# A two-block fp32 transformer kernel: sums with a 0/1 matrix as split fp32r products, both heads of a pair side by side

## The chip, the core and the metric

One Trainium2 chip, one of its cores. The metric is the device time of one execution of the whole program, in microseconds (us); the kernel before took 2313.67 us, the median of three runs (2313.24 to 2315.27).

## The reference, cut to what matters

Two layers of a first block (feed-forward, mixer, feed-forward), then two layers of a second block that the change doesn't touch. The sequence is 256 tokens, the width 1024, with 8 heads of 128. The mixer has two branches. The delta branch runs a gated delta rule and norms its output per head:

```python
o_a = gated_delta_rule_chunked(q, k, v, g, beta).transpose(0, 2, 1, 3)
o_a = rmsnorm(o_a, dn_out_norm) * jax.nn.silu(dn_z...)
```

The stick branch is an attention whose weights need, for each query, a sum over the keys behind each key:

```python
log_1mb = jnp.where(causal, -jax.nn.softplus(z), 0.0)
survive = lax.cumsum(log_1mb, axis=3, reverse=True) - log_1mb
weights = jnp.where(causal, jnp.exp(jax.nn.log_sigmoid(z) + survive), 0.0)
```

All arithmetic has the accuracy of fp32. Weights of products are cut in two fp32r parts (high and low, `hi` and `lo`), and a product is three matmuls of parts.

## The kernel before, in words

**Queues.** SyncE loads weight units of 1 MB into a ring of three buffers `raw`. ScalarE copies each into `hi` in fp32r (L1313), GpSimd subtracts and writes `lo`, four instructions of 128x512 a unit (L539), and TensorE multiplies. Each engine has one order of work, written out by hand, and waits on semaphores.

**Mixer.** The dependent steps of the delta rule and of the stick branch are short, so TensorE fills the time between them with parts of weight units: a unit is 48 matmuls of 256 columns and is cut in four parts of 12. `DELTA_PLAN` and `SB_PLAN` say how many parts stand behind which step; they are computed from the weights `DELTA_WEIGHT` and `SB_WEIGHT`. In the stick branch the steps of one pair of heads are `z` (scores), `tri` (sums) and `pv` (output). Pair 0 has 12 parts behind `z` and 8 behind `tri`; pairs 1, 2 and 3 have 3 behind each `z`, and 2, 3 and 2 behind `tri`; none stands behind `pv`.

**Stick, one pair.** TensorE writes the scores of head i to bank 4 + i (L938, L939). ScalarE takes the absolute value, Exp and Ln (L1520 to L1522). VectorE forms max(z, 0) + soft (L2152) and multiplies with a mask of 0 and -1 (`sbneg`, L2153), 768 columns each, and signals `nsp`. TensorE does the square sums of the next pair (`pre`, L794), waits for `nsp`, and adds the sums: per head three fp32 matmuls of 256, 128 and 128 columns with the 0/1 matrices `tri` and `ones` stationary (L948 to L950). VectorE then forms the exponent (L2157), ScalarE does Exp (L1535), TensorE the output (L958, L959).

**Delta, output norm, one pair.** There are four pairs a layer. ScalarE squares the output into `sq` (L1500), VectorE adds a term (L2133) and signals `osq`. TensorE sums over partitions with `ones` in fp32, two matmuls of 256 columns (L839), the first thing of the next pair's work on TensorE. ScalarE takes the root (L1460). On VectorE `started` stands behind L2133 (L2061, L2064), then the steps of the next pair.

An fp32 matmul is two records in the trace, each with a weight load. The helper `halve` cuts a tile in two fp32r parts: a copy (L1916), a wait for it, a subtraction (L1917).

```python
def halve(h, l_, src):
    own.link(V.tensor_copy(h, src))
    return tt(l_, src, h.bitcast(F32), ALU.subtract)
```

Of the kernel before, what the change touches and what calls it, by code (L numbers as in the profile page):

```python
# [25 lines left out]
P = 128  # L26
D = 1024
S = 256
# [37 lines left out]
          "sbneg", "sbadd", "cosa", "sina", "cosb", "sinb", "scan"]  # L66
CONST_W = {**{f"inv{n}": 64 for n in range(6)}, "half": 64, "sbneg": 384, "sbadd": 384, "cosa": 256, "sina": 256, "cosb": 256, "sinb": 256, "scan": 256}
# [194 lines left out]
def build_program(nc, a, const, out):  # L262
    ctx = ExitStack()
    with ctx:
# [36 lines left out]
        beta_r, g_r, eg_r = (sb(n, [HEADS, S]) for n in ("beta_r", "g_r", "eg_r"))  # L301
# [244 lines left out]
        def _(pe):  # L546
# [424 lines left out]
            def mixer1(l, b, q):  # L971
# [24 lines left out]
                for n, row in enumerate((beta_r[:, :], g_r[:, :], sq[0:HEADS, 0, 0:S], sq[0:HEADS, 1, S:2 * S])):  # L996
# [307 lines left out]
        def _(act):  # L1304
# [203 lines left out]
            def stick(l, c):  # L1508
# [11 lines left out]
                own.link(fn(soft.rearrange("p (i n) -> p i n", i=2), ps[:, 4:6, 0:384], ACT.Abs))  # L1520
# [366 lines left out]
        def _(dve):  # L1887
# [134 lines left out]
            def delta(l):  # L2022
# [60 lines left out]
                for c in range(NPAIR):  # L2083
# [49 lines left out]
                    tt(o2, o2, ps[:, 6:8, S:2 * S], ALU.add).then_inc(dl_dve, 1)  # L2133
# [44 lines left out]
            def mixer1(l, b):  # L2178
                h8 = slice(0, HEADS)
                y, e = sq[h8, 0, 0:S], sq[h8, 0, S:2 * S]  # L2180
                gates = ps[h8, A_AT % 2, S:2 * S]
# [378 lines left out]
```

## Time and profile before

| | |
|---|---|
| median of three runs | 2313.67 us |
| the profiled execution, from its first to its last instruction | 2311.9 us |
| TensorE matmul busy | 2261.3 us, 98% |
| TensorE weight load busy | 2061.2 us, 89% |
| VectorE busy | 1068.2 us, 46% |
| ScalarE busy | 1090.0 us, 47% |
| GpSimd busy | 1698.7 us, 73% |
| granted TensorE clock, mean | 0.999 of full speed |

The span stands 1.8 us below the median: what lies around the instructions isn't in the profile. PE is a matmul, PEld a weight load, DVE is VectorE, ACT ScalarE, POOL GpSimd. In brackets behind a row stands the idle time of its engine just before it, and whose work ended it. Matmuls are pipelined: the spacing of their starts tells what one costs, not its duration.

### The profile page before, as it was taken

What the parts mean: (1) busy time and instruction counts of PE and PEld (TensorE: products, weight loads), DVE (VectorE), ACT (ScalarE), POOL (GpSimd) and SP (SyncE); (2) the same over time, 40 slices, a digit from 0 to 9 for tenths busy, and PEclk for the clock granted to TensorE, in tenths of its full rate; (3) what the DMA queues carried; (4) which work ended last, traced back from release to release, by engine and by line L of the source; (5) the groups of instructions that cost most, each with busy time, mean ns of one, the idle gap of its engine ahead of it and who ended that gap; (6) DMA issues with size and microseconds to landing.
All of it is one profiled execution on the core that took longest, in us unless ns stands there. A gap on an engine that the chain in (4) does not pass through costs nothing.

```text
span 2311.9 us, 41644 instructions
## 1 busy us (share of the span) xinstructions
PE 2261.3 (98%) x16621; PEld 2061.2 (89%) x16621; DVE 1068.2 (46%) x1873; ACT 1090.0 (47%) x1319; POOL 1698.7 (73%) x1340
## 2 busy tenths in 40 slices
PE   8999999999999999999999999999999999999998
PEld 7888999999988888898999998889898888898887
DVE  3334656323333333365553233333635765534766
ACT  4335444465433533454444734345654335565333
POOL 6998655556799899874554678996567997555996
PEclk9999999999999999999999999999999999999999
DMA  7554533334565555543333445664334555333553
GB/s 239 192 197 148 165 110 111 119 101 146 166 200 186 178 193 188 190 156 108 108 118 108 142 158 176 193 208 137 110 121 143 191 187 180 117 104 119 198 197 119
DMA packets 312365, 359.91 MB, mean 156 GB/s; under 512 B 18660, under 2 KB 291104, under 8 KB 312096
## 3 DMA queue, kind: packets, MB, share of 16 engines
q1 hardware_dynamic: 311866, 357.59, 47.6%
q8 instruction: 102, 1.67, 0.3%
q10 hardware_dynamic: 358, 0.33, 0.0%
q14 instruction: 39, 0.32, 0.0%
HBM read 356.84 MB, written 1.05 MB: 155 GB/s over the span
## 4 chain that ended last, share of the span: by engine, by line
PE 89%; DVE 6%; ACT 3%; POOL 1%; issue 1%; DMA 0%; SPq 0%; ACTq 0%; DVEq 0%
PE ps L755 23%; PE ps L566 21%; PE ps L598 17%; PE ps L603 9%; PE ps L632 4%; PE ps L885 1%; PE ps L867 1%; PE ps L1154 1%; PE ps L648 1%; POOL sb_lo L539 1%; PE ps L888 1%; PE ps L619 1%; PE ps L1206 1%; PE ps L794 1%; PE ps L989 1%
## 5 line engine op out<-in xcount | busy, mean ns | idle before, releaser
L539 POOL TENSOR_TENSOR sb_lo<-sb_raw,sb_hi 128x512 fp32r<-128x512 f32 (+1 forms) x1336 | 1698.5, 1306 | 594.9 <-ACT sb_hi L1313 593.5
L1313 ACT ACTIVATE sb_hi<-sb_raw 128x2048 fp32r<-128x2048 f32 (+3 forms) x341 | 639.4, 1877 | 740.2 <-PE ps L603 358.4
L598 PE MATMUL ps<-sb_hT,sb_hi 128*128 128x512 f32 x1792 | 426.0, 390 | 0.0
L598 PEld LDWEIGHTS ps<-sb_hT,sb_hi 128*128 128x128 f32 x1792 | 332.7, 188 | 66.7
L755 PE MATMUL ps<-sb_hT,sb_hi 128*128 128x256 f32 x2304 | 309.0, 287 | 4.5 <-DVE sb_hT L2162 2.8
L755 PEld LDWEIGHTS ps<-sb_hT,sb_hi 128*128 128x128 f32 x2304 | 284.9, 191 | 10.6 <-DVE sb_hT L2162 3.2
L603 PEld LDWEIGHTS ps<-sb_hT,sb_lo 128*128 128x128 f32 x1792 | 229.8, 191 | 8.7
L1910 DVE TENSOR_TENSOR sb_yinv<-ps,sb_row 128x512 f32<-128x512 f32 x112 | 77.5, 692 | 337.2 <-PE ps L603 336.4
L603 PE MATMUL ps<-sb_hT,sb_lo 128*128 128x256 f32 x1792 | 232.4, 283 | 0.0
L566 PE MATMUL ps<-sb_hi,sb_o_h 128*128 128x512 f32 x560 | 219.8, 392 | 0.4 <-DVE sb_o_l L1917 0.4
L566 PE MATMUL ps<-sb_hi,sb_o_l 128*128 128x512 f32 x560 | 218.7, 390 | 0.0
L566 PE MATMUL ps<-sb_lo,sb_o_h 128*128 128x512 f32 x560 | 218.0, 389 | 0.0
L755 PE MATMUL ps<-sb_hT,sb_lo 128*128 128x256 f32 x1152 | 158.2, 285 | 0.0
L755 PEld LDWEIGHTS ps<-sb_hT,sb_lo 128*128 128x128 f32 x1152 | 145.5, 191 | 1.3
L566 PEld LDWEIGHTS ps<-sb_lo,sb_o_h 128*128 128x128 f32 x560 | 105.1, 188 | 22.4
L566 PEld LDWEIGHTS ps<-sb_hi,sb_o_h 128*128 128x128 f32 x560 | 105.4, 188 | 21.0 <-DVE sb_o_l L1917 0.8
L566 PEld LDWEIGHTS ps<-sb_hi,sb_o_l 128*128 128x128 f32 x560 | 105.4, 188 | 19.2
L1904 DVE TENSOR_TENSOR ps<-ps,sb_row 128x512 f32<-128x512 f32 x134 | 92.7, 692 | 52.6 <-PE ps L566 19.0
L1916 DVE CAST sb_o_h<-ps 128x512 fp32r<-128x512 f32 x82 | 56.7, 691 | 107.8 <-PE ps L566 105.1
L566 PE MATMUL ps<-sb_hT,sb_hi 128*128 128x256 f32 (+1 forms) x520 | 96.3, 284 | 3.2 <-issue 2.0
L632 PE MATMUL ps<-sb_hT,sb_hi 128*128 128x256 f32 x448 | 90.3, 294 | 7.9 <-DVE sb_hT L1898 7.7
L566 PEld LDWEIGHTS ps<-sb_hT,sb_hi 128*128 128x128 f32 (+1 forms) x520 | 80.6, 187 | 4.6 <-issue 4.5
(402 smaller groups left out, 3355.5 us busy)
## 6 DMA issues: line engine op xcount, KB each, us to landing
sb_raw<-in_ffn_w_in SPq DMA_DIRECT2D x88, 1024.0 KB, 5.1
sb_raw<-in_w_in SPq DMA_DIRECT2D x78, 1024.0 KB, 5.2
sb_raw<-in_ffn_w_out SPq DMA_DIRECT2D x44, 1024.0 KB, 4.9
sb_raw<-in_ffn_w_up SPq DMA_DIRECT2D x44, 1024.0 KB, 5.1
sb_raw<-in_ffn_w_down SPq DMA_DIRECT2D x22, 1024.0 KB, 4.9
sb_raw<-in_w_out SPq DMA_DIRECT2D x16, 1024.0 KB, 5.2
sb_raw<-in_w_branch_a SPq DMA_DIRECT2D x8, 1024.0 KB, 5.1
sb_raw<-in_w_branch_b SPq DMA_DIRECT2D x8, 1024.0 KB, 5.2
```

Of the source, the lines that this page charges most:

```text
L539: ins = nc.gpsimd.tensor_tensor(lo[:, slot, c], raw[:, slot, c], hi[:, slot, c].bitcast(F32), ALU.subtract)
L566: ins = mm(dst, s, m, start=first and n == 0, stop=last and n == 3 * len(pairs) - 1)
L598: mm(ps[:, bank + i, :].rearrange("p (h n) -> p h n", h=2), wh[:, c, i * P:(i + 1) * P], hT_both[:, :, c, :], start=c == 0, stop=False, sk ...
L603: ins = mm(ps[:, bank + i, 0:S], wl[:, c, i * P:(i + 1) * P], hT_h[:, c, :], start=False, stop=c == KB - 1, skip_group_check=True)
L619: ins = nc.tensor.transpose(ps[:, bank, i * S + t * P:i * S + (t + 1) * P], x[:, t, k * P:(k + 1) * P], ident)
L632: ins = mm(ps[:, bank, i * S:(i + 1) * S], wt[:, c, i * P:(i + 1) * P], h[:, c, :], start=(i, c, n) == (0, 0, 0), stop=(c, n) == (KB - 1, ...
L648: ins = mm(ps[:, bank, t * S:(t + 1) * S], o[:, (c + UNSCALED_AT) % KB, tt_], wt[:, c, :], start=(t, c, n) == (0, 0, 0), stop=(c, n) == (K ...
L755: ins = mm(dst, left, right, start=at == 0, stop=of_low and k == KB - 1, skip_group_check=True)
L1313: fn(hi[:, slot, 0:width], raw[:, slot, 0:width], ACT.Copy).then_inc(hi_ready, 1)
L1904: return tt(v, v, over(row[:], 2), ALU.mult)
L1910: tt(t, low, over(row[:], 2), ALU.mult)
L1916: own.link(V.tensor_copy(h, src))
```

## The change

The stationary matrices become `-tri` and `-ones` in fp32r (`signs`, made once from the constants). The moving operand is cut by `halve` into two fp32r parts of 768 columns (`parts`), both heads of a pair side by side, so that one matmul serves both heads: for a pair two of 512 columns and four of 256 take the place of the six fp32 ones. The sign sits in the stationary matrix, so the mask is 0/1 (`before`), and VectorE multiplies only the two diagonal blocks of each head, 256 columns an instruction. The scores of a pair are laid out flat over banks 4 and 5; the number of their matmuls stays. L2157 becomes two instructions, of 512 and of 256 columns. The output sums of the delta branch are cut in the same way: `halve` over 512 columns, then four fp32r matmuls of 256 columns for two fp32 ones. To make room, `beta_r`, `g_r`, `eg_r` and the scan mask move into `quad`; the scan mask is made by three memsets a layer, and 640 columns of constants are no longer loaded.

```diff
@@ output sums, TensorE
                     for i in range(2):
-                        ins = mm(ps[:, 6 + i, S:2 * S], cc("ones"), sq[:, 0, i * S:(i + 1) * S], start=True, stop=True)
+                        for j in range(2):
+                            ins = mm(ps[:, 6 + i, S:2 * S], minus_ones, parts[:, j, i * S:(i + 1) * S], start=j == 0, stop=j == 1)
@@ stick, TensorE
                 wv("nsp")
-                for i in range(2):
-                    n0 = rsf[:, 384 * i:384 * i + S]
-                    n1 = rsf[:, 384 * i + S:384 * (i + 1)]
-                    mm(ps[:, 4 + i, 0:S], cc("tri"), n0, start=False, stop=False, skip_group_check=True)
-                    mm(ps[:, 4 + i, P:S], cc("ones"), n1, start=False, stop=False, skip_group_check=True)
-                    ins = mm(ps[:, 4 + i, S:S + P], cc("tri"), n1, start=False, stop=True, skip_group_check=True)
+                early, late = parts[:, :, 0:512], parts[:, :, 512:768]
+                behind = ps[:, 4, :].rearrange("p (i n) -> p i n", i=2)[:, :, P:S]
+                for j in range(2):
+                    mm(ps[:, 4, :], minus_tri, early[:, j, :], start=False, stop=False, skip_group_check=True)
+                for j in range(2):
+                    mm(behind, minus_ones, late[:, j, :].rearrange("p (i n) -> p i n", i=2), start=False, stop=j == 1, skip_group_check=True)
+                for j in range(2):
+                    ins = mm(ps[:, 5, 0:S], minus_tri, late[:, j, :], start=False, stop=j == 1, skip_group_check=True)
@@ output sums, VectorE
-                    tt(o2, o2, ps[:, 6:8, S:2 * S], ALU.add).then_inc(dl_dve, 1)
+                    own.link(tt(o2, o2, ps[:, 6:8, S:2 * S], ALU.add))
+                    halve(parts[:, 0, 0:512], parts[:, 1, 0:512], sq[:, 0, :]).then_inc(dl_dve, 1)
@@ stick, VectorE
-                own.link(stt(out=pair(neg), in0=ps[:, 4:6, 0:384], scalar=0.0, in1=pair(soft), op0=ALU.max, op1=ALU.add))
-                tt(pair(neg), pair(neg), over(cc("sbneg"), 2), ALU.mult).then_inc(sb_dve, 1)
+                own.link(stt(out=rate, in0=ps[:, 4:6, :].rearrange("p b n -> p (b n)")[:, 0:768], scalar=0.0, in1=soft, op0=ALU.max, op1=ALU.add))
+                for square in (pair(rate[:, 0:512])[:, :, 0:P], pair(rate[:, 512:768])):
+                    ins = tt(square, square, over(cc("before"), 2), ALU.mult)
+                own.link(ins)
+                halve(parts[:, 0, :], parts[:, 1, :], rate).then_inc(sb_dve, 1)
@@ mixer1, VectorE
+                own.link(V.memset(scan, 1.0))
+                for c in range(S // CHUNK):
+                    ins = V.memset(scan[:, c * CHUNK:c * CHUNK + 1], 0.0)
+                own.link(ins)
...
+                if l == 0:
+                    for i, name in enumerate(("tri", "ones")):
+                        ts(signs[:, i, :], cc(name), -1.0, None, ALU.mult)
```

## Rows read from the trace of the kernel before

**Rows 1.** The page, busy time of each engine over the span.

```profile
PE 2261.3 (98%) x16621; PEld 2061.2 (89%) x16621; DVE 1068.2 (46%) x1873; ACT 1090.0 (47%) x1319; POOL 1698.7 (73%) x1340
```

**Rows 2.** The chain that ended last: start us, us, what, and how many instructions.

```profile
51.57 3.65 PE ps L598 x16
...
582.22 5.76 PE ps L781 x48
```

**Rows 3.** Timeline of TensorE, stick stage, first layer: start us, us, engine, line, operation.

```profile
524.46 0.59 PE L948 MATMUL ps<-sb_rs,sb_const 128*128 128x256 f32 x2
...
526.13 1.68 PE L755 MATMUL ps<-sb_o_h,sb_lo 128*128 128x256 f32 x12
...
537.74 0.59 PE L948 MATMUL ps<-sb_rs,sb_const 128*128 128x256 f32 x2
...
551.30 0.70 PE L948 MATMUL ps<-sb_rs,sb_const 128*128 128x256 f32 x2 [0.40 <-DVE sb_rs L2153]
```

**Rows 4.** Timeline of VectorE, the same stage.

```profile
522.29 1.23 DVE L2153 TENSOR_TENSOR sb_rs<-sb_rs,sb_const 128x768 f32<-128x768 f32 x1
...
535.57 0.96 DVE L2153 TENSOR_TENSOR sb_rs<-sb_rs,sb_const 128x768 f32<-128x768 f32 x1
...
550.29 0.96 DVE L2153 TENSOR_TENSOR sb_rs<-sb_rs,sb_const 128x768 f32<-128x768 f32 x1
```

**Rows 5.** Timeline of GpSimd, the same stage.

```profile
518.90 10.73 POOL L539 TENSOR_TENSOR sb_lo<-sb_raw,sb_hi 128x512 fp32r<-128x512 f32 x8
...
530.13 5.03 POOL L539 TENSOR_TENSOR sb_lo<-sb_raw,sb_hi 128x512 fp32r<-128x512 f32 x4 [0.51 <-ACT sb_hi L1313]
...
551.14 5.00 POOL L539 TENSOR_TENSOR sb_lo<-sb_raw,sb_hi 128x512 fp32r<-128x512 f32 x4 [2.73 <-ACT sb_hi L1313]
```

**Rows 6.** One line's instructions: times, ns min/median/max, first and last start.

```profile
L2055 DVE TENSOR_TENSOR sb_levels<-sb_levels,sb_const x16: 418/1341/1550, 265.2 to 1206.5; 64x256 f32<-64x256 f32 x16
```

**Rows 7.** Groups of VectorE's instructions by shape, 1600 to 1660 us.

```profile
L1917 DVE TENSOR_TENSOR sb_hT<-sb_zT,sb_hT 128x768 fp32r<-128x768 f32 x1 | 1.0, 959 | 0.0
...
L1916 DVE CAST sb_hT<-sb_zT 128x768 fp32r<-128x768 f32 x1 | 0.6, 559 | 0.0
```

**Rows 8.** Timeline of TensorE at the output sums of pairs 0 to 3.

```profile
316.55 1.13 PE L839 MATMUL ps<-sb_sq,sb_const 128*128 128x256 f32 x4 [0.47 <-DVE sb_sq L2133]
...
372.00 1.06 PE L839 MATMUL ps<-sb_sq,sb_const 128*128 128x256 f32 x4
...
433.06 1.03 PE L839 MATMUL ps<-sb_sq,sb_const 128*128 128x256 f32 x4
...
484.26 1.03 PE L839 MATMUL ps<-sb_sq,sb_const 128*128 128x256 f32 x4
```

**Rows 9.** Timeline of VectorE at the same four places.

```profile
315.81 0.69 DVE L2133 TENSOR_TENSOR sb_sq<-sb_sq,ps 128x512 f32<-128x512 f32 x1
...
371.19 0.69 DVE L2133 TENSOR_TENSOR sb_sq<-sb_sq,ps 128x512 f32<-128x512 f32 x1
...
430.75 0.69 DVE L2133 TENSOR_TENSOR sb_sq<-sb_sq,ps 128x512 f32<-128x512 f32 x1
...
480.49 0.69 DVE L2133 TENSOR_TENSOR sb_sq<-sb_sq,ps 128x512 f32<-128x512 f32 x1 [2.98 <-ACT sb_sq L1500]
```

**Rows 10.** Timeline of GpSimd at three of them.

```profile
311.52 5.40 POOL L539 TENSOR_TENSOR sb_lo<-sb_raw,sb_hi 128x512 fp32r<-128x512 f32 x4 [6.97 <-ACT sb_hi L1313]
...
369.53 5.46 POOL L539 TENSOR_TENSOR sb_lo<-sb_raw,sb_hi 128x512 fp32r<-128x512 f32 x4 [0.49 <-ACT sb_hi L1313]
...
484.75 1.29 POOL L539 TENSOR_TENSOR sb_lo<-sb_raw,sb_hi 128x512 fp32r<-128x512 f32 x1 [3.21 <-ACT sb_hi L1313]
```

**Rows 11.** Timeline of VectorE, start of the mixer, first layer.

```profile
210.96 1.66 DVE L2187 SCALAR_TENSOR_TENSOR sb_qT<-ps,sb_vec,sb_row 128x256 f32<-128x256 f32 x4 [2.36 <-ACT sb_row L1355]
...
222.81 0.88 DVE L1988 TENSOR_SCALAR sb_qT<-ps,sb_vec 128x256 f32<-128x256 f32 x2 [3.94 <-PE ps L989]
```

**Rows 12.** Sums of a stretch: us, busy of each engine, granted clock, DMA share, GB/s.

```profile
1640.00:1650.00 10.00, 8.61 (x54) 7.74 (x53) 8.53 (x17) 5.38 (x19) 7.52 (x5) 0.83 0.43 135
```

More of the change, by code:

```diff
@@ L65 @@
 CONSTS = ["ident", "ones", "halves", "tri", "rot", "chunk", "half", "inv0", "inv1", "inv2", "inv3", "inv4", "inv5",
-          "sbneg", "sbadd", "cosa", "sina", "cosb", "sinb", "scan"]
-CONST_W = {**{f"inv{n}": 64 for n in range(6)}, "half": 64, "sbneg": 384, "sbadd": 384, "cosa": 256, "sina": 256, "cosb": 256, "sinb": 256, "scan": 256}
+          "before", "sbadd", "cosa", "sina", "cosb", "sinb"]
+CONST_W = {**{f"inv{n}": 64 for n in range(6)}, "half": 64, "sbadd": 256, "cosa": 256, "sina": 256, "cosb": 256, "sinb": 256}
 CONST_AT, _w = {}, 0
@@ L98, in constants @@
     before = (j < i).astype(np.float32)
-    full = np.concatenate([before, np.ones((P, P), np.float32), before], axis=1)
-    put("sbneg", -full)
-    put("sbadd", np.where(full > 0, 0.0, -1e30).astype(np.float32))
+    put("before", before)
+    put("sbadd", np.concatenate([np.where(before > 0, 0.0, -1e30), np.zeros((P, P))], axis=1).astype(np.float32))
     def table(d_rot):
@@ L300, in build_program @@
         vec2 = sb("vec2", [P, 3 * P])
-        beta_r, g_r, eg_r = (sb(n, [HEADS, S]) for n in ("beta_r", "g_r", "eg_r"))
+        beta_r, g_r, eg_r, scan = (quad[0:HEADS, i, 0:S] for i in range(4))
+        signs = sb("signs", [P, 2, P], F32R)
+        minus_tri, minus_ones = (signs[:, i, :] for i in range(2))
+        parts = sb("parts", [P, 2, 768], F32R)
         select = sb("select", [P, HEADS], F32R)
@@ L954, in stick @@
                 for i, h in enumerate(heads):
-                    w0 = sqf[:, 384 * i:384 * i + S]
-                    w1 = sqf[:, 384 * i + S:384 * (i + 1)]
+                    w0 = sqf[:, i * S:(i + 1) * S]
+                    w1 = sqf[:, 512 + i * P:512 + (i + 1) * P]
                     hh = slice(h * P, (h + 1) * P)
@@ L995, in mixer1 @@
                 pe.wait_ge(rows_dve, ROWS_DVE.at(l, "beg"))
-                for n, row in enumerate((beta_r[:, :], g_r[:, :], sq[0:HEADS, 0, 0:S], sq[0:HEADS, 1, S:2 * S])):
+                for n, row in enumerate((beta_r, g_r, sq[0:HEADS, 0, 0:S], sq[0:HEADS, 1, S:2 * S])):
                     for t in range(ST):
@@ L1459, in output_roots @@
                     act.wait_ge(dl_pe, DELTA_PE.at(NPAIR * l + c, "osum"))
-                    own.link(fn(two(rs[:, 0, :]), ps[:, 6:8, S:2 * S], ACT.Ln, bias=eps_t[:, 1:2], scale=1.0 / P))
+                    own.link(fn(two(rs[:, 0, :]), ps[:, 6:8, S:2 * S], ACT.Ln, bias=eps_t[:, 1:2], scale=-1.0 / P))
                     fn(rs[:, 0, :], rs[:, 0, :], ACT.Exp, scale=-0.5).then_inc(dl_act, 1)
@@ L1518, in stick @@
                 wp("z")
-                own.link(fn(soft.rearrange("p (i n) -> p i n", i=2), ps[:, 4:6, 0:384], ACT.Abs))
+                own.link(fn(soft, ps[:, 4:6, :].rearrange("p b n -> p (b n)")[:, 0:768], ACT.Abs))
                 own.link(fn(soft, soft, ACT.Exp, scale=-1.0))
@@ L2203, in mixer1 @@
                 freed(l, B_AT)
-                own.link(tt(beta_r[:, :], beta_r[:, :], cc("ones")[h8, 0:1].to_broadcast([HEADS, S]), ALU.add))
-                own.link(V.reciprocal(beta_r[:, :], beta_r[:, :]))
+                own.link(tt(beta_r, beta_r, cc("ones")[h8, 0:1].to_broadcast([HEADS, S]), ALU.add))
+                own.link(V.reciprocal(beta_r, beta_r))
                 dve.wait_ge(rows_act, ROWS_ACT.at(l, "ln"))
@@ L2209, in mixer1 @@
                 own.link(ts(gates, gates, hcol[:, 2:3], -1.0, ALU.mult, ALU.mult))
-                own.link(V.tensor_tensor_scan(out=g_r[:, :], data0=cc("scan")[h8, :], data1=gates, initial=0.0, op0=ALU.mult, op1=ALU.add))
+                own.link(V.tensor_tensor_scan(out=g_r, data0=scan, data1=gates, initial=0.0, op0=ALU.mult, op1=ALU.add))
                 dve.sem_inc(bank_free[A_AT % 2], 1)
-                gc = g_r[:, :].rearrange("h (c n) -> h c n", n=CHUNK)
+                gc = g_r.rearrange("h (c n) -> h c n", n=CHUNK)
                 tt(d.rearrange("h (c n) -> h c n", n=CHUNK), gc[:, :, CHUNK - 1:CHUNK].to_broadcast([HEADS, S // CHUNK, CHUNK]), gc,
```

20 lines of the change are left out of this document (10 added, 10 removed).

## The prediction

> **What bounds the kernel now.** I read the page first: TensorE is busy 98% of the span and GpSimd 73%, VectorE and ScalarE under half [rows 1]. So a microsecond that leaves TensorE's order of work leaves the time, provided that nobody makes TensorE wait. The edit moves work the other way too: out of TensorE, into VectorE, and in two places where TensorE waits for exactly the result of that VectorE work. So the question is how much room stands between the moment when VectorE is ready and the moment when TensorE gets there. I read that from the timelines of TensorE and VectorE laid side by side, at the stick sums [rows 3, 4] and at the output sums [rows 8, 9], and then that of GpSimd in the same stretches [rows 5, 10], for a reason that comes below. The second layer repeats the first within 0.1 us in all of these, so I work out one layer and double it.
>
> **What TensorE gains.** The sums of one stick pair run from 524.46 to 526.13 [rows 3]: 1.67 us for 1024 fp32 columns (two heads of 256 + 128 + 128), so 1.63 ns a column. In fp32r a matmul of 512 columns costs 3.65 / 16 = 0.228 us and one of 256 costs 5.76 / 48 = 0.120 us [rows 2]. The new sums are 2 x 0.228 + 4 x 0.120 = 0.94 us, 0.73 less. The output sums are 512 fp32 columns, 0.83 us, and become 4 x 0.120 = 0.48 us, 0.35 less. With four stick pairs and four delta pairs in each of two layers that is 8 x (0.73 + 0.35) = 8.6 us. The scores keep their matmuls and cost nothing new.
>
> **What VectorE gains in work.** Between the combined tile and the signal `nsp` stood one product of 768 columns, 0.96 us [rows 4]. Now there are two products of 256 columns, at 0.42 us each (the shortest of L2055, same count of columns [rows 6]), a cast of 768 columns from SBUF to SBUF, 0.56 us, and a subtraction of 768 columns, 0.96 us [rows 7], with three waits of some 0.03 us: 2.45 us, 1.46 more. At the output sums a cast and a subtraction of 512 columns are added: some 0.5 us (between the 0.42 of 256 columns and the 0.56 of 768) and 0.69 us as for L2133 [rows 9], with two waits 1.25 us.
>
> **What these instructions meet.** They differ from most of VectorE's in one thing: none of their operands is in PSUM. L2055 is such an instruction, and it takes 418 ns at best, 1341 in the median, 1550 at most [rows 6]. L2153 is one too: 0.96 us in pairs 2 and 3 and 1.23 in pair 1 [rows 4]. GpSimd works without a break from 518.90 to 529.63, and is idle when the two short ones start: one run of it ends at 535.16, the next begins at 551.14 [rows 5]. In steps of 1.25 us (5.03 / 4), the third GpSimd instruction after 518.90 ends at 522.7, and L2153 ends 0.8 us behind that, at 523.52, which is its own 768 columns. So a VectorE instruction that lives in SBUF alone waits for the end of the running GpSimd instruction and then needs its columns; the next GpSimd instruction then waits for it, and the next VectorE one for that. Two of L2055 in a row cost 1.4 us each in this way, for 0.42. The Trainium skill (SBUF — State Buffer, who interferes with whom) has this as a rule: the two engines share a pair of ports under an exclusive lock, taken by VectorE instructions with two SBUF inputs and by copies and casts in the two-port mode, and whoever is second blocks. It speaks against this change, and the trace agrees, with 418 against 1341 ns; for a cast beside GpSimd no row here shows it. By that rule the sum is the +15.0 us below; with casts left out of it, some 1.4 us a meeting less.
>
> **Stick sums, pair by pair.** Pair 0 has 12 parts of filler behind `z`, over ten us, so VectorE's extra work is hidden and 0.73 is gained. In pair 1 the products are issued at 522.29, or 0.73 sooner by that gain, but they meet the same GpSimd instruction, since its run doesn't move. The first ends at 522.7 + 0.28 = 522.98, the second one GpSimd instruction later at 524.4, the cast at 526.0, the subtraction at 528.06. TensorE was there at 524.46: it starts 3.65 us later, and 0.73 comes off: +2.9 for pairs 0 and 1 together. In pair 2 GpSimd is idle, VectorE is done at 535.53 + 2.45 = 537.98, TensorE was there at 537.74: +0.3 - 0.73 = -0.43. In pair 3 the products and the start of the cast are free (550.29 to 551.1), GpSimd starts at 551.14 behind the cast, and the subtraction waits for its first instruction (to 552.9) and ends at 553.7; TensorE started at 551.30 and waited already: +2.45 - 0.73 = +1.7. One layer: +4.2 us. L2157 as two instructions reads PSUM, so no lock; it is at most 0.1 us longer, and 2 or 3 parts of filler cover it.
>
> **Output sums.** L2133 ends at 316.50, 371.88, 431.44 and 481.18 [rows 9], TensorE starts at 316.55, 372.00, 433.06 and 484.26 [rows 8]. In the first the cast meets the last of four GpSimd instructions (to 316.92 [rows 10]), ends at 317.19, and the subtraction is free, to 317.92: +1.42 - 0.35 = +1.07. In the second GpSimd is in the middle of its four (369.53 to 374.99), both meet it, cast to 372.58 and subtraction to 374.30: +2.35 - 0.35 = +2.0. The third has the same pattern with 1.6 us of room: ready at 433.9, +0.9 - 0.35 = +0.55. In the fourth GpSimd is idle until 484.75 and there are 3 us of room: -0.35. `started` comes later by as much, but 2 or 3 parts of filler stand between TensorE's next steps and its result. One layer: +3.3 us.
>
> **The small edits.** The memsets stand before a wait in which VectorE was idle for 2.36 us, the two negations before one of 3.94 us [rows 11], even at one GpSimd instruction each (2 x 1.3). Both are hidden; without that cover they'd cost 3 us once. The rows in `quad` keep their instructions. 640 columns of constants less are 0.33 MB that TensorE doesn't wait for: nothing.
>
> **Sum.** (4.2 + 3.3) x 2 = +15.0 us. The profiled span goes from 2311.9 to 2326.9, the median, 1.8 above it, from 2313.67 to 2328.7.
>
> **Rivals.** *No meeting:* casts and fp32r results don't take the lock, or VectorE gets it first. Then pair 1 costs +0.24 - 0.73, pair 3 +1.45 - 0.73, pairs 0 and 2 as above, together -0.9; the output sums +0.9, +0.83, -0.35, -0.35, together +1.0. Two layers: +0.2, 2313.9 us, no change. For it: no cast beside GpSimd is in the trace. Against it: the subtractions have the form of L2153, which did wait.
> *All hidden,* the side opposite to mine: VectorE's work ends inside the filler, and TensorE's 8.6 us come through whole, 2305.1 us. It decides at rooms of 1.5 us in the stick sums and 1.25 us in the output sums. The rooms are over ten us only in stick pair 0; 0.95, 1.2 and 0.05 us in the others; 0.05, 0.1, 1.6 and 3.1 us at the output sums. It would need a filler or a VectorE chain that is other than the trace has it.
> *The clock falls:* in 1640 to 1650 us TensorE was busy for 8.61 of 10 us with short pieces, and the granted clock was 0.83 in the mean [rows 12], so a third of it at 1.2 GHz, worth 1.7 us. A stall of 3.65 us in pair 1 of each layer could bring the same: 3.4 us more, 2332.1.
>
> **Numbers.** Forecast 0.60, no meeting 0.18, all hidden 0.11, clock 0.11. A measurement of this kernel can tell 0.2% from no change, 4.6 us. Slower by more than that: 0.60 + 0.11 = 0.71; within: 0.18; faster: 0.11. The likeliest case's own range is 2320 to 2334 (one meeting more or less per layer and place is 1.3 us). To hold 8 in 10 the range reaches down to the case of no meeting, 2312, and up to 2336 for the clock.
>
> **What the profile would show.** L1916 and L1917 in the stick stage at 0.56 and 0.96 in pair 2, and 1.3 to 2.1 us in pair 1; TensorE idle before the first sum by some 3.6 us in pair 1, 0.2 in pair 2, 2.5 in pair 3, released by VectorE's subtraction; before the output sums by 1.4 to 2.4 us in pairs 0 and 1. The sums themselves 0.94 us instead of 1.67. I'd be wrong if casts run beside GpSimd at 0.56, or if TensorE's idle time there is under 1 us.

## The result, and the profile after

The change makes the kernel slower: 2339.35 us, the median of four runs (2336.64 to 2341.29), against 2314.47 for the kernel before in runs beside it (2313.24 to 2315.86), a ratio of 1.0104 [1.0092 to 1.0115]. That is 25 us more; the forecast was 15, and 2339.35 lies above the range. Two single executions of kernels further down took far longer than their others (5720.61 and 2761.25 us) and are left out of all comparisons; the first was the profiled one of the last kernel of experiment 3, so there are no rows of it.

The page of the kernel after, the span and the busy time of each engine (beside [rows 1]):

```profile
span 2337.9 us, 41603 instructions
...
PE 2265.2 (97%) x16573; PEld 2064.4 (88%) x16573; DVE 1109.4 (47%) x1929; ACT 1089.3 (47%) x1319; POOL 1705.2 (73%) x1340
```

The span grew by 26.0 us. TensorE is busy for 3.9 us more although it was given less to do, and its share fell from 98% to 97%. VectorE has 41 us more, GpSimd 6.5. So two questions: where TensorE waits now, and why it is busy for longer.

The waits of TensorE after: who waits for whom, us in total, times, the longest.

```profile
PE ps L950 <- DVE sb_parts L1921: 13.7, 4, 4.1
PE ps L841 <- DVE sb_parts L1921: 9.4, 6, 2.2
PE ps L633 <- DVE sb_hT L1902: 8.0, 12, 2.6
```

The first two rows are new and are the two places of the change, both released by the subtraction of `halve` (L1921, L1917 before): 23.1 us. Before, the same two places waited for 0.8 and 0.9 us (0.40 and 0.47 a layer [rows 3, 8]), so 21.4 us are new. The next row was 7.7 us before and is 8.0, and of the others none has changed by more than 0.5 us.

The timeline of TensorE, the sums of the stick pairs 1, 2 and 3 and the output sums of the delta pairs 0 to 3, first layer (start us, us, engine, line, operation, in brackets the idle time before it and who ended it); these answer to [rows 3, 8]:

```profile
534.35 1.22 PE L950 MATMUL ps<-sb_parts,sb_signs 128*128 128x512 f32 x2 [4.10 <-DVE sb_parts L1921]
...
548.55 0.73 PE L950 MATMUL ps<-sb_parts,sb_signs 128*128 128x512 f32 x2
...
549.59 0.28 PE L756 MATMUL ps<-sb_o_h,sb_hi 128*128 128x256 f32 x1
...
563.73 0.73 PE L950 MATMUL ps<-sb_parts,sb_signs 128*128 128x512 f32 x2 [2.73 <-DVE sb_parts L1921]
```

```profile
318.24 0.74 PE L841 MATMUL ps<-sb_parts,sb_signs 128*128 128x256 f32 x4 [1.88 <-DVE sb_parts L1921]
...
377.11 1.23 PE L841 MATMUL ps<-sb_parts,sb_signs 128*128 128x256 f32 x4 [2.15 <-DVE sb_parts L1921]
...
440.14 0.74 PE L841 MATMUL ps<-sb_parts,sb_signs 128*128 128x256 f32 x4 [0.69 <-DVE sb_parts L1921]
...
491.06 0.64 PE L841 MATMUL ps<-sb_parts,sb_signs 128*128 128x256 f32 x4
```

Waits of 4.10, 0.06 (the gap to the end of the matmuls before) and 2.73 us, and of 1.88, 2.15, 0.69 and 0 us. The second layer has the same within 0.02 us. Now the starts against those of before: the seven are later by 1.69, 5.11, 7.08, 6.80, 9.89, 10.81 and 12.43 us, in the order of time. From the third output sums to the fourth, where nobody waits, the kernel gains 0.28 us, as meant. But from the second to the third it loses 1.97 us, of which the wait explains 0.69, and from stick pair 1 to pair 2 it loses 0.92 us with a wait of only 0.06. Something else is lost behind a wait. The sums of stretches show what (us, busy time of PE, PEld, DVE, ACT, POOL with counts, granted clock, DMA share, GB/s):

```profile
300.00:318.00 18.00, 16.35 (x141) 16.15 (x139) 8.75 (x15) 12.49 (x26) 10.21 (x8) 1.00 0.19 60
318.00:323.00 5.00, 4.76 (x36) 4.52 (x37) 1.54 (x4) 3.12 (x3) 0.76 (x1) 0.66 0.65 210
323.00:377.00 54.00, 51.95 (x594) 49.26 (x592) 33.38 (x66) 21.57 (x33) 29.01 (x24) 1.00 0.32 99
377.00:381.00 4.00, 3.89 (x29) 3.55 (x30) 2.49 (x4) 2.60 (x3) 1.18 (x1) 0.57 0.38 103
381.00:534.00 153.00, 148.56 (x1525) 139.69 (x1523) 69.96 (x120) 77.97 (x93) 91.07 (x71) 1.00 0.38 120
534.00:538.00 4.00, 3.65 (x17) 3.47 (x17) 1.84 (x4) 0.49 (x1) 2.66 (x2) 0.57 0.32 102
538.00:564.00 26.00, 23.21 (x167) 21.19 (x166) 13.12 (x20) 16.07 (x17) 12.79 (x10) 1.00 0.39 121
564.00:569.00 5.00, 5.00 (x29) 4.92 (x29) 1.62 (x3) 0.85 (x1) 3.30 (x3) 0.66 0.10 20
569.00:700.00 131.00, 128.97 (x880) 119.92 (x879) 44.34 (x70) 53.75 (x47) 109.57 (x87) 1.00 0.53 175
```

From the end of each wait TensorE works without a break to 323, 381, 538 and 569, but these four stretches are at a granted clock of 0.57 to 0.66: a piece of 3.4 us in each at half speed, 1.2 instead of 2.4 GHz, and full speed in the other stretches of the table. The four pieces begin at 319.1, 377.1, 534.1 and 564.8, from 0.3 us before to 1.1 us behind the end of the waits of 1.88, 2.15, 4.10 and 2.73 us; at the one of 0.69 us there is none. Up to the last matmul it is 30.7 us at half clock: seven pieces of 3.4 us in the two mixers (three in the second layer, at 1165.6, 1322.6 and 1353.3) and one of 6.8 us at 2039.4, in the second block; the kernel before has one piece of 3.4 us, the one in [rows 12], and that one is gone after. Half speed for 27.3 us more costs at most 13.7 us. (The first 18 us are left out here and below: there a matmul of 256 columns costs 0.21 us instead of 0.12 in every kernel, but only some traces list the half clock.) Not every piece belongs to the change: the traces of all the kernels further down have some in the second block, which no edit touches, at places that differ from one to the next. So the clocks of all the timed executions are the better measure: 0.9930 in the mean of the four of this kernel, 0.9979 in the 48 of the kernel before that were run for the experiments. The difference, times 2338 us, is some 11.5 us at most; a single execution's clock is rounded to 0.001, or 2.3 us.

VectorE in stick pairs 1 and 2, and GpSimd beside it (beside [rows 4, 5]):

```profile
527.90 2.93 DVE L2159 TENSOR_TENSOR sb_rs<-sb_rs,sb_const 128x256 f32<-128x256 f32 x2
530.86 1.50 DVE L1920 CAST sb_parts<-sb_rs 128x768 fp32r<-128x768 f32 x1
532.39 1.90 DVE L1921 TENSOR_TENSOR sb_parts<-sb_rs,sb_parts 128x768 fp32r<-128x768 f32 x1
...
546.15 0.76 DVE L2159 TENSOR_TENSOR sb_rs<-sb_rs,sb_const 128x256 f32<-128x256 f32 x2
546.94 0.56 DVE L1920 CAST sb_parts<-sb_rs 128x768 fp32r<-128x768 f32 x1
547.54 0.96 DVE L1921 TENSOR_TENSOR sb_parts<-sb_rs,sb_parts 128x768 fp32r<-128x768 f32 x1
...
561.18 0.56 DVE L1920 CAST sb_parts<-sb_rs 128x768 fp32r<-128x768 f32 x1
561.78 1.90 DVE L1921 TENSOR_TENSOR sb_parts<-sb_rs,sb_parts 128x768 fp32r<-128x768 f32 x1
```

```profile
520.36 16.30 POOL L540 TENSOR_TENSOR sb_lo<-sb_raw,sb_hi 128x512 fp32r<-128x512 f32 x12 [6.12 <-ACT sb_hi L1317]
...
553.58 5.00 POOL L540 TENSOR_TENSOR sb_lo<-sb_raw,sb_hi 128x512 fp32r<-128x512 f32 x4 [8.07 <-ACT sb_hi L1317]
561.24 6.06 POOL L540 TENSOR_TENSOR sb_lo<-sb_raw,sb_hi 128x512 fp32r<-128x512 f32 x4 [2.66 <-ACT sb_hi L1317]
```

In pair 1 GpSimd runs from 520.36 to 536.66 without a break, and the two products take 2.93 us, the cast 1.50 and the subtraction 1.90. In pair 2 GpSimd is idle and they take 0.76, 0.56 and 0.96. In pair 3 it starts at 561.24, behind the cast's start, and only the subtraction is long, 1.90. That is the forecast's mechanism, seen in all three forms.

**Where the 26.0 us of the span come from:** +21.4 new waits; -6.8 matmuls (a block of stick sums takes 1.04 us instead of 1.67, from 548.55 to 549.59 in pair 2 against 524.46 to 526.13 [rows 3], but only 0.33 less in pair 0; the output sums take 0.2 to 0.4 less a pair; so 2 x (3 x 0.63 + 0.33) + 8 x 0.3 = 6.8); the rest, +11.4, is a remainder that I put down to the clock, which could account for up to 13.7 by this trace and 11.5 by the timed clocks.

### The profile page after: what moved, and what is told of

Same layout as the page of the kernel before. It is cut to its first block, busy times and chain, and to the rows that moved or that the text cites. A ratio compares the mean times of both kernels' runs of the same rounds, so it can differ in the third digit from the quotient of the medians.

```text
span 2337.9 us, 41603 instructions
## 1 busy us (share of the span) xinstructions
PE 2265.2 (97%) x16573; PEld 2064.4 (88%) x16573; DVE 1109.4 (47%) x1929; ACT 1089.3 (47%) x1319; POOL 1705.2 (73%) x1340
## 3 DMA queue, kind: packets, MB, share of 16 engines
q8 instruction: 102, 1.67, 0.3%
## 4 chain that ended last, share of the span: by engine, by line
PE 84%; DVE 8%; ACT 5%; issue 1%; POOL 1%; DMA 0%; SPq 0%; ACTq 0%; DVEq 0%
PE ps L567 21%; PE ps L756 20%; PE ps L599 17%; PE ps L604 9%; PE ps L633 4%; PE ps L887 1%; PE ps L869 1%; PE ps L1158 1%; PE ps L649 1%; POOL sb_lo L540 1%; PE ps L890 1%; DVE sb_parts L1921 1%; PE ps L620 1%; ACT sb_hi L1317 1%; DVE sb_levels L2059 1%
## 5 line engine op out<-in xcount | busy, mean ns | idle before, releaser
L756 PEld LDWEIGHTS ps<-sb_hT,sb_hi 128*128 128x128 f32 x2304 | 287.0, 193 | 10.7 <-DVE sb_hT L2171 3.2
L1920 DVE CAST sb_o_h<-ps 128x512 fp32r<-128x512 f32 x82 | 56.7, 691 | 107.8 <-PE ps L567 105.1
```

Of the source, the lines that this page charges most:

```text
L756: ins = mm(dst, left, right, start=at == 0, stop=of_low and k == KB - 1, skip_group_check=True)
```

## The experiments

All ratios are to the kernel before, run beside them on the same chip (2315.08 to 2315.68 us in the four groups of runs), with a 95% interval.

**1. The two parts, each alone.** The change without its output-sum part:

```diff
-  for j in range(2):
-      ins = mm(ps[:, 6 + i, S:2 * S], minus_ones, parts[:, j, i * S:(i + 1) * S], start=j == 0, stop=j == 1)
+  ins = mm(ps[:, 6 + i, S:2 * S], cc("ones"), sq[:, 0, i * S:(i + 1) * S], start=True, stop=True)
...
-  own.link(tt(o2, o2, ps[:, 6:8, S:2 * S], ALU.add))
-  halve(parts[:, 0, 0:512], parts[:, 1, 0:512], sq[:, 0, :]).then_inc(dl_dve, 1)
+  tt(o2, o2, ps[:, 6:8, S:2 * S], ALU.add).then_inc(dl_dve, 1)
```

> The change without its output-sum part. Theory (port lock plus a slower clock behind the stalls): TensorE waits before the stick sums as in the whole change, some 13.7 us in four waits, gains 8 x 0.73 = 5.8 us, and the clock falls behind the waits of pairs 1 and 3, four times at 1.3 to 1.7 us: 2314.5 + 13 to 15 = 2328 to 2330 us. Rival (the rest of the 25 us comes from the new layout or from matmuls that are dearer than forecast, no clock): +8 us, 2322 us, or +13 with no stretch of lower clock in the trace.

Measured: 2327.51 us (2326.23 to 2331.17), ratio 1.0058 [1.0042 to 1.0075]. The waits for L1920 are 13.6 us in 4, the longest 4.1, as in the whole change, and the trace has 10.2 us at half clock (behind the wait of pair 1 in each layer, not of pair 3, and once in the second block). The reverse, the kernel before with the output-sum part alone:

```diff
-  ins = mm(ps[:, 6 + i, S:2 * S], cc("ones"), sq[:, 0, i * S:(i + 1) * S], start=True, stop=True)
+  for j in range(2):
+      ins = mm(ps[:, 6 + i, S:2 * S], minus_ones[:, :], parts[:, j, i * S:(i + 1) * S], start=j == 0, stop=j == 1)
...
-  tt(o2, o2, ps[:, 6:8, S:2 * S], ALU.add).then_inc(dl_dve, 1)
+  own.link(tt(o2, o2, ps[:, 6:8, S:2 * S], ALU.add))
+  halve(parts[:, 0, 0:512], parts[:, 1, 0:512], sq[:, 0, :]).then_inc(dl_dve, 1)
```

> The kernel before with the output-sum part alone. Theory: waits of 1.9, 2.2 and 0.7 us before the output sums of pairs 0 to 2 in each layer, less 0.35 us for each of eight sums, plus up to three falls of the clock at 1.3 to 1.7 us: +10 to +12, 2325 to 2327 us; this and the stick part alone add up to the 25 us of the whole. Rival (no clock): +6.5 us, 2321 us.

Measured: 2325.38 us (2324.24 to 2326.49), 1.0045 [1.0028 to 1.0061]; 9.4 us of waits in 6, 13.7 us at half clock. So +12.2 and +10.1 us: both parts lose, each by more than its new waits (13.6 - 0.8 and 9.4 - 0.9) less its gain (4.4 and 2.4), which would be +8.4 and +6.1. With the time at half clock over the 3.4 us of before, at half its length, they are at most +11.8 and +11.2. They nearly add up: 22.3 against 24.9. Both times lie where the theory put them or just below, and well above the rivals without a clock, 2322 and 2321 us.

**2. Is it the clock?** If the remainder is the clock's, work that TensorE does *while it would wait anyway* must make the kernel faster, with no result ready sooner. First in the kernel after, ahead of the wait of stick pairs 1 and 3, with transposes whose result nobody reads:

```diff
+  for _ in range((0, 24, 0, 12)[c]):
+      nc.tensor.transpose(ps[:, 7, 0:P], ident, ident)
   wv("nsp")
```

> The change with idle matmuls (24 transposes in pair 1, 12 in pair 3 of the stick stage, into a bank nobody uses) ahead of the wait for the parts, so that TensorE's idle time there falls from 4.1 and 2.7 us to some 1.2 us while the results come no sooner. Theory (the clock falls because TensorE idles): the four falls of the clock behind the stick sums go away, 5 to 7 us less than the change, 2333 us. Rival (the clock isn't what costs; the waits are all): the same time as the change, 2339 us.

Measured: 2334.22 us (2328.69 to 2337.62), 1.0087 [1.0070 to 1.0104]; 5.1 us less than the change, but the intervals overlap. TensorE's timeline and the sum of 526 to 570 in the profiled execution, the fastest of the four:

```profile
527.89 2.78 PE L947 MATMUL ps<-sb_const 128*128 128x128 f32 x24
532.20 0.73 PE L952 MATMUL ps<-sb_parts,sb_signs 128*128 128x512 f32 x2 [1.53 <-DVE sb_parts L1923]
...
526.00:570.00 44.00, 39.58 (x286) 35.79 (x286) 23.64 (x31) 23.35 (x23) 26.58 (x20) 1.00 0.41 135
```

The wait is cut in two, 2.78 us of work and 1.53 idle, and the clock in this stage is 1.00, where the change has 0.93 in 526 to 572. The four timed clocks are 0.994 to 0.997, 0.9955 in the mean against 0.9930; the 0.0025 more are worth 6 us at most, about what was gained. But the falls behind the output sums can stay, and they come and go: one in this trace, three in that of the change. A cleaner pair was needed.

**3. VectorE's work without TensorE's gain.** The kernel before, where VectorE also cuts the masked tile in two parts that nobody reads, before it signals; the sums stay in fp32:

```diff
-  tt(pair(neg), pair(neg), over(cc("sbneg"), 2), ALU.mult).then_inc(sb_dve, 1)
+  own.link(tt(pair(neg), pair(neg), over(cc("sbneg"), 2), ALU.mult))
+  halve(parts[:, 0:768], parts[:, 768:1536], neg).then_inc(sb_dve, 1)
```

> The kernel before, all its matmuls kept; only VectorE makes the two parts of the stick sums as well (a cast and a subtraction of 768 columns ahead of the signal), which nobody reads. Theory: TensorE waits 2.6 us in pair 1, 0.4 in pair 2 and 3.7 in pair 3, in two layers 13 us less the 0.8 of before, and the clock falls behind some of the waits of pairs 1 and 3 (up to four times 1.7 us): 2315 + 12.5 + 2 to 6 = 2330 to 2334 us. Rival (the time comes from the new matmuls and the layout, not from VectorE's work): 2315 to 2320 us.

Measured: 2336.62 us (2336.06 to 2338.56), 1.0095 [1.0080 to 1.0111], over the expected 2330 to 2334. The waits are 2.43, 0.25 and 3.90 us a layer in pairs 1 to 3 (expected 2.6, 0.4, 3.7); the clock took more than I allowed. TensorE in pair 3 and the stretch around it:

```profile
558.30 1.22 PE L949 MATMUL ps<-sb_rs,sb_const 128*128 128x256 f32 x2 [3.90 <-DVE sb_quad L1918]
...
556.00:564.00 8.00, 5.70 (x25) 5.34 (x26) 3.76 (x4) 0.85 (x1) 4.59 (x3) 0.57 0.33 109
```

At this wait the fall lasts 6.8 us; it begins at 556.4, 1.9 us before the wait ends. The waits of 2.43 us in pair 1 have none. In all 23.9 us at half clock, of which 10.2 lie away from the stick sums. Now the same with transposes ahead of the wait in pairs 1 and 3:

```diff
+  for _ in range((0, 14, 0, 22)[c]):
+      nc.tensor.transpose(ps[:, 7, 0:P], ident, ident)
```

> The same with idle matmuls ahead of the two long waits (14 in pair 1, 22 in pair 3, some 0.12 us each), so that TensorE idles about 1 us there. Theory: results come no sooner, but the clock stays up: 2 to 6 us less than without them. Rival (clock doesn't matter): the same time, or more.

Measured: 2330.36 us (2328.46 to 2333.12), 1.0062 [1.0047 to 1.0078]: 6.3 us *less*, with 72 transposes *more* and VectorE's instructions the same; the two intervals don't touch. The granted clock of the timed executions is 0.9972 in the mean against 0.9935, worth up to 8.8 us. This shows that the wait costs more than its length, and that the clock is what it costs. (That VectorE's results come no sooner is read from the program; no rows show it.)

**4. What the lock costs, and how to get around it.** In the kernel after with the sum of squares left in PSUM, so that the add, the cast and the subtraction each have an operand there:

```diff
-  own.link(tt(o2, o2, ps[:, 6:8, S:2 * S], ALU.add))
-  halve(parts[:, 0, 0:512], parts[:, 1, 0:512], sq[:, 0, :]).then_inc(dl_dve, 1)
+  summed = ps[:, 6:8, S:2 * S]
+  own.link(tt(summed, o2, summed, ALU.add))
+  halve(two(parts[:, 0, 0:512]), two(parts[:, 1, 0:512]), summed).then_inc(dl_dve, 1)
```

> The change with the output norm's sum of squares left in PSUM, so that cast and subtraction read PSUM: 0.69 us each, not shorter than before, but with an operand outside SBUF. Theory (VectorE instructions in SBUF alone wait for GpSimd): ready 1.45 us behind L2137 in all pairs whatever GpSimd does; the waits before the output sums are 1.4, 1.3 and 0 us instead of 1.9, 2.2 and 0.7, so 4 us less in two layers, and up to three falls of the clock fewer: 2331 to 2335 us. Rival (the instructions are simply long): no change, or slower by the longer cast.

Measured: 2334.03 us (2331.50 to 2334.22), 1.0078 [1.0061 to 1.0095]; the intervals of this kernel and the change just overlap, the times don't. The cast and the subtraction at the second output sums in the change, then VectorE and TensorE at the same place in this kernel, GpSimd busy beside both:

```profile
374.70 0.69 DVE L1920 CAST sb_parts<-sb_sq 128x512 fp32r<-128x512 f32 x1
375.42 1.63 DVE L1921 TENSOR_TENSOR sb_parts<-sb_sq,sb_parts 128x512 fp32r<-128x512 f32 x1
...
371.98 1.85 DVE L2059 TENSOR_TENSOR sb_levels<-sb_levels,sb_const 64x256 f32<-64x256 f32 x2
373.87 0.69 DVE L2138 TENSOR_TENSOR ps<-sb_sq,ps 128x512 f32<-128x512 f32 x1
374.60 0.69 DVE L1920 CAST sb_parts<-ps 128x512 fp32r<-128x512 f32 x1
375.32 0.69 DVE L1921 TENSOR_TENSOR sb_parts<-ps,sb_parts 128x512 fp32r<-128x512 f32 x1
...
376.07 0.74 PE L841 MATMUL ps<-sb_parts,sb_signs 128*128 128x256 f32 x4 [1.21 <-DVE sb_parts L1921]
```

Out of PSUM both take 0.69 us, beside 1.85 for two small instructions in SBUF just before them. The subtraction gains 0.94 us, and the wait falls by as much. The cast gains nothing: it is slower out of PSUM (with GpSimd idle it takes 0.43 us from SBUF, in the first kernel of experiment 7), and in the change it met only the end of a GpSimd instruction. The wait falls from 2.15 to 1.21 us, the third to 0. The first is 1.91 and not 1.4: I had forgotten the 0.47 us that the kernel before waits there [rows 8].

**5. The high part first.** Without the output-sum part, and with a signal of its own for the high part, so that TensorE multiplies it while VectorE subtracts:

```diff
-  wv("nsp")
   for j in range(2):
+      wv(("hi", "nsp")[j])
       mm(ps[:, 4, :], minus_tri, early[:, j, :], start=False, stop=False, skip_group_check=True)
-  for j in range(2):
       mm(behind, minus_ones, late[:, j, :].rearrange("p (i n) -> p i n", i=2), start=False, stop=j == 1, skip_group_check=True)
-  for j in range(2):
       ins = mm(ps[:, 5, 0:S], minus_tri, late[:, j, :], start=False, stop=j == 1, skip_group_check=True)
...
-  halve(parts[:, 0, :], parts[:, 1, :], rate).then_inc(sb_dve, 1)
+  V.tensor_copy(parts[:, 0, :], rate).then_inc(sb_dve, 1)
+  dve.wait_ge(sb_dve, SB_DVE.at(g, "hi"))
+  tt(parts[:, 1, :], rate, parts[:, 0, :].bitcast(F32), ALU.subtract).then_inc(sb_dve, 1)
```

> The stick part of the change, with a signal of its own for the high part, so that TensorE does the three matmuls of the high part while VectorE subtracts. Theory: in pair 1 the high part is ready 1.9 us and in pair 3 1.9 us ahead of the low one, so TensorE starts that much sooner but then waits for the low part; what it saves is the 0.5 us of the high part's matmuls in pairs 1 to 3 and the long idle time is cut in two shorter ones, so fewer falls of the clock: 1.5 x 2 = 3 us less, and 2 to 5 us of clock: 2320 to 2325 us. Rival (waits are all that counts): 2325 us.

Measured: 2325.48 us (2323.85 to 2326.27), 1.0047 [1.0032 to 1.0062], just above what was expected, at the rival's 2325, and only 2.0 less than without the split.

```profile
PE ps L949 <- DVE sb_parts L2157: 5.9, 4, 2.2
PE ps L949 <- DVE sb_parts L2159: 4.0, 4, 1.2
```

9.9 us of waits instead of 13.6. In this trace 17.1 us are at half clock instead of 10.2: at the two shorter waits with little work between them (2.17 and 0.84 us in pair 1) the clock was down for 6.8 us in each layer. But the timed clocks are the same, 0.9952 in the mean against 0.9950 in the four executions without the split. So the split took 3.7 us off the waits, and the clock that the expectation had hoped to win with it didn't come; that the split cost clock isn't shown.

**6. No products on the path.** As 5, and the mask is added to the scores by TensorE (identity stationary, a mask of -1e30 and 0 moving, both fp32r), so that masked scores give zero in `rate` without a product, and the later add of a mask falls away too:

```diff
+  mm(ps[:, 4, :].rearrange("p (i n) -> p i n", i=2)[:, :, 0:P], ident_r, over(mask_r, 2), start=False, stop=False, skip_group_check=True)
+  ins = mm(ps[:, 5, 0:S].rearrange("p (i n) -> p i n", i=2), ident_r, over(mask_r, 2), start=False, stop=False, skip_group_check=True)
...
-  for square in (pair(rate[:, 0:512])[:, :, 0:P], pair(rate[:, 512:768])):
-      ins = tt(square, square, over(cc("before"), 2), ALU.mult)
...
-  stt(out=pair(soft[:, 0:512]), in0=pair(ps[:, 4, :]), scalar=0.0, in1=over(cc("sbadd"), 2), op0=ALU.min, op1=ALU.add)
-  stt(out=pair(soft[:, 512:768]), in0=pair(ps[:, 5, 0:S]), scalar=0.0, in1=over(cc("sbadd")[:, 0:P], 2), op0=ALU.min, op1=ALU.add).then_inc(sb_dve, 1)
+  ts(soft, ps[:, 4:6, :].rearrange("p b n -> p (b n)")[:, 0:768], 0.0, None, ALU.min).then_inc(sb_dve, 1)
```

> As the split one, and the mask is added to the scores by TensorE (identity stationary, -1e30 moving, two fp32r matmuls of 256 columns) so that VectorE has no products to do: its chain is the combined tile, cast, subtraction. The output sums are those of before. Theory: the high part is ready before TensorE comes in pairs 1 and 2 and about with it in pair 3, the low one within 0.3 us (at most 1.4 in pair 3) of the end of the high part's matmuls; per layer the sums save 4 x 0.6 us, the mask costs 4 x 0.24, the wait of 0.4 in pair 3 goes: 0.4 to 1.6 us less than before a layer, 2312 to 2314 us against 2315, and no new fall of the clock. Rival (the lock holds the cast and the subtraction up by two GpSimd instructions in pairs 1 and 3): +2 us a layer, 2319 us.

Measured: 2312.64 us (2311.12 to 2314.58, 11 runs) against 2315.68, 0.9990 [0.9981 to 0.9999]. It is the only version ahead of both kernels, by 0.1%, which is less than the 0.2% named in the prediction. TensorE in stick pair 1 and VectorE in pairs 1 and 3:

```profile
523.79 0.80 PE L950 MATMUL ps<-sb_parts,sb_signs 128*128 128x512 f32 x1
...
525.43 0.50 PE L950 MATMUL ps<-sb_parts,sb_signs 128*128 128x512 f32 x1 [0.61 <-DVE sb_parts L2157]
...
526.01 1.59 PE L755 MATMUL ps<-sb_o_h,sb_lo 128*128 128x256 f32 x12
...
522.00 1.43 DVE L2155 CAST sb_parts<-sb_rs 128x768 fp32r<-128x768 f32 x1
523.47 1.91 DVE L2157 TENSOR_TENSOR sb_parts<-sb_rs,sb_parts 128x768 fp32r<-128x768 f32 x1
...
549.74 0.56 DVE L2155 CAST sb_parts<-sb_rs 128x768 fp32r<-128x768 f32 x1
550.33 0.96 DVE L2157 TENSOR_TENSOR sb_parts<-sb_rs,sb_parts 128x768 fp32r<-128x768 f32 x1
```

The cast still meets GpSimd (1.43 us), but it is the first thing behind the combined tile and ends before TensorE gets there; only the low part is late, by 0.61 us, and 3.4 us are at half clock, as before the change. With one signal for both parts:

```diff
-  wv(("hi", "nsp")[j])
...
+  wv("nsp")
```

> The kernel with the mask on TensorE, but one signal for both parts, as in the change. Theory: in pair 1 the low part is ready some 0.9 us behind TensorE's arrival, in pair 3 some 1.5 us; all idle times stay under 1.6 us, so no fall of the clock behind them: (0.9 + 1.5) x 2 less the 0.5 us of overlap that the split gave each pair 1 and 3, so 3 to 4 us more than with the split, 2316 us, clock 0.997 to 0.999. Rival (most of the gain comes from the split): 2320 us or more.

Measured: 2315.12 us, 0.9994 [0.9984 to 1.0004], no difference from before; waits of 1.07 and 0.99 us a layer, 4.1 in all. So some 12 us go when the products leave the path: the waits are 9.5 us shorter than with the stick part alone (13.6 to 4.1), the timed clock is 0.9979, that of the kernel before, instead of 0.9950 (up to 6.7 us), and the mask's matmuls cost something back (0.24 us a pair, 1.9 in all, by the expectation's estimate). The split seems to be worth some 2 us here, though the two intervals overlap.

**7. The output sums in this version.** First a kernel whose add takes `sq` twice, so that its query term is left out; it makes the add, the cast and the subtraction three SBUF instructions in a row (on TensorE the two matmuls of the high part wait for `ohi`, those of the low part for `osq`):

```diff
-  own.link(tt(o2, o2, ps[:, 6:8, S:2 * S], ALU.add))
-  halve(parts[:, 0, 0:512], parts[:, 1, 0:512], sq[:, 0, :]).then_inc(dl_dve, 1)
+  own.link(tt(osum, o2, osum, ALU.add))
+  V.tensor_copy(two(parts[:, 0, 0:512]), osum).then_inc(dl_dve, 1)
+  dve.wait_ge(dl_dve, DELTA_DVE.at(g, "ohi"))
+  tt(two(parts[:, 1, 0:512]), osum, two(parts[:, 0, 0:512]).bitcast(F32), ALU.subtract).then_inc(dl_dve, 1)
```

> The kernel with the mask on TensorE and the split signal, and the output sums as in the change, with a split signal too (four fp32r matmuls of 256 columns, the high ones while VectorE subtracts). Theory: the waits at the output sums are 1.1 and 0.4 us in pair 0, 0.6 and 1.4 in pair 1, 0 and 0.6 in pair 2, none long enough for the clock to fall; per layer +0.8, +1.7, +0.25 and -0.35 us, so 4.8 us more than with fp32 output sums, 2317 us, where the same part in one wait cost 10 us. Rival (the clock falls by the sum of the idle time, not by one long piece): 2321 to 2323 us.

Measured: 2334.88 us, 1.0083 [1.0066 to 1.0099], far over the expectation; waits of 1.88, 2.14 and 0.68 us a layer ahead of the high part, 23.9 us at half clock. The cast takes 0.43 us at the first and the fourth output sums and 1.37 to 1.39 at the second and third. Then with the add of the kernel before, which reads PSUM:

```diff
-  own.link(tt(osum, o2, osum, ALU.add))
+  own.link(tt(o2, o2, ps[:, 6:8, S:2 * S], ALU.add))
```

> The output sums as fp32r parts with a split signal, this time with the add of the query term as in the change (its second operand in PSUM). Theory: the cast is ready 0.7 us behind the add, the subtraction 0.7 us later where GpSimd is idle and 1.6 us later where it works; the waits at the output sums are two short ones (at most 1.2 and 1.4 us) in place of one of 1.9 to 2.1, so the clock doesn't fall behind them; +0.8, +1.7, +0.25 and -0.35 us a layer: 4.8 us over the kernel with the mask on TensorE, 2317 us, clock 0.997 to 0.998. Rival (the clock falls by the sum of the idle time, not by one long piece): 2321 to 2323 us, clock 0.995 to 0.996.

Measured: 2322.60 us (2317.86 to 2325.09, 10 runs), 1.0029 [1.0019 to 1.0039]. One operand moved from SBUF to PSUM is worth 12.3 us here, by the lock and the clock together. Yet it is 10 us over the version without the output-sum part. VectorE and TensorE at the second output sums, and what follows:

```profile
374.67 0.68 DVE L2138 CAST sb_parts<-sb_sq 128x512 fp32r<-128x512 f32 x1
375.38 1.64 DVE L2140 TENSOR_TENSOR sb_parts<-sb_sq,sb_parts 128x512 fp32r<-128x512 f32 x1
...
375.40 0.50 PE L840 MATMUL ps<-sb_parts,sb_signs 128*128 128x256 f32 x2 [0.49 <-DVE sb_parts L2138]
377.08 0.50 PE L840 MATMUL ps<-sb_parts,sb_signs 128*128 128x256 f32 x2 [1.18 <-DVE sb_parts L2140]
...
371.00:377.50 6.50, 4.83 (x38) 4.30 (x36) 6.32 (x8) 1.80 (x2) 6.02 (x5) 1.00 0.51 161
377.50:381.00 3.50, 3.50 (x28) 3.37 (x28) 1.87 (x3) 3.12 (x3) 0.81 (x2) 0.51 0.44 118
```

Waits of 0.49 and 1.18 us, with 0.5 us of work between them, and then the clock at 0.51; in pair 0 it is the same behind waits of 1.19 and 0.23 us. I had expected no fall behind waits this short, since in the mixers single waits of 1.2 to 1.6 us had brought none. The time and the clock are those of the expectation's rival (2321 to 2323 us); by what rule the clock falls the trace doesn't say. Of the 10 us, 6.2 are waits (3.4 + 3.7, less 0.9 in the kernel before), less the gain of 2.4. The trace has 17.1 us at half speed against 3.4, up to 6.9 us, but two of its five pieces (at 1036.3 and 1742.8) stand where the version without the output-sum part and without the split has them too, and by the timed clocks (0.9963 against 0.9974) it is up to 2.5 us. So some 3.7 us of the 10 stay unexplained.

## Why the prediction was wrong

- **The lock.** Right, in mechanism and in size. The forecast's new waits are 4.4 (3.65, and the 0.73 by which TensorE comes sooner), 0.3, 2.45 and 1.42, 2.35, 0.9, 0 us a layer, together 11.8. Measured, less the waits of before: 4.10, 0.06, 2.33 and 1.41, 2.15, 0.69, 0, together 10.7. The cast beside GpSimd, for which no row stood, is 1.50 us and doesn't run at 0.56, so the rival without meetings falls. The Trainium skill (SBUF — State Buffer, who interferes with whom) puts casts in the two-port mode under the exclusive lock as well. The trace agrees, with 1.50 against 0.56 us. The sum's +23.6 was +21.4.
- **TensorE's gain.** Right in sign, 6.8 us instead of 8.6. The block of stick sums is 1.04 us and not 0.94. In pair 0 it is 1.34 in the trace, and the output sums gain 0.2 to 0.4 and not always 0.35.
- **The clock: the step that failed.** The sum has no term for it. It stood among the rivals at 0.11 and was mis-sized there: "two falls", one behind pair 1 of each layer, 3.4 us. There were seven in the mixers, and one in the second block: behind pair 3 and behind the output sums too, where I had myself forecast waits of 1.4 to 2.5 us and never asked what they'd do to the clock. The remainder of 11.4 us, 11.5 at most by the timed clocks, is over three times the rival's price. The row that I had [rows 12] shows a fall in a stretch of short pieces whose longest wait is 1.11 us; from it I took the price of one fall, and applied it to my longest wait alone. The miss in the span is +11.0 us: -2.2 for the waits, +1.8 for the gain, +11.4 for this.
- **All hidden.** Refuted: room enough was only in stick pair 0 and at the fourth output sums, as said. The small edits cost nothing that shows: TensorE is 0.3 us later when the mixer starts.
- **The range** reached to 2336, some 4 us over the sum with one fall a layer (2332.1); its upper end left out the case that the sum and several falls come together. The sign was right for the reason given, the lock: the new waits alone are three times TensorE's gain.

What stays open: how much idle time brings a fall. In the mixers of the six traces whose waits are single ones, 19 of the 30 waits of 1.88 us or more had one, and the same place can have it in one trace and not in the next (2.73 us in pair 3: yes in the change, no with the stick part alone). Whether the fall at 2039.4 in the second block belongs to the change was not tried; it begins 2.4 us behind a wait of 1.11 us that the kernel before has too.

## What to carry to other kernels

Where TensorE is at 98%, price a wait that you add by its length and by the clock behind it, up to 1.7 us for each piece of 3.4 us at half speed; here one wait of 2 us a layer with a fall behind it would have spent TensorE's whole gain of 3.4. Before you move work to VectorE, ask for each instruction whether an operand lies in PSUM and what GpSimd does at that moment: a cast of 512 columns took 0.43, up to 1.39 or, out of PSUM, 0.69 us, a subtraction 0.69, 1.63 or 0.69. And when a step must be added on a path, look for what can leave that path (here the mask's product, by a cheap matmul while TensorE has the bank anyway): that turned +12 us into no difference, and with the split signal into -3.

## What was not expected of the hardware

- The granted clock fell to half at 19 of 30 single waits of 1.88 to 4.12 us, for 3.4 or 6.8 us, and also behind waits of 0.49 and 1.18 us that stand 0.5 us apart.
- Useless work in the wait made the kernel faster: 2330.36 us with it, 2336.62 without.
- A cast from SBUF to SBUF waits for GpSimd like a product with two operands in SBUF does: 1.42 to 1.54 us for 768 columns instead of 0.56. A subtraction of 768 columns takes 1.90 to 1.94 instead of 0.96.
- Which GpSimd instruction a cast meets, and when, decides: 512 columns took 0.43 us alone, 0.60 to 0.69 in the change and 1.37 to 1.39 behind an add in SBUF.
- GpSimd pays as well: four of its instructions take 5.00 to 5.03 us alone and 6.06 in the run that meets a subtraction.
- In the page the busy time of TensorE *rose* by 3.9 us while its work shrank: the busy share doesn't tell a slow clock from work.
